# Padding the rows of the two stationary buffers of a float32r matmul kernel, from 256 to 272 and 260 columns a block

## What is computed

```python
u = rms_norm(x, norm_pre_mix)
proj = u @ w_in                                   # 2048 x 8512
q_sb, k_sb, v_sb, q_lat, kv_lat, k_r, gate_logits = split(proj)
y_sb  = stick_breaking_attention(q_sb, k_sb, v_sb) @ w_o_sb
y_mla = mla_attention(rms_norm(q_lat) @ w_uq, rms_norm(kv_lat) @ w_ukv, k_r) @ w_o_mla
mixed = (g_sb * y_sb + g_mla * y_mla) @ w_out     # g_* = sigmoid(gate_logits + b_gate)
h = x + rms_norm(mixed)
gu = rms_norm(h) @ w_gate_up                      # 2048 x 11264
h = h + rms_norm((silu(g) * up) @ w_down)         # 5632 x 2048
...
x = layer_norm(ALPHA * h + attention_mixer(h))    # h @ a_w_in, attention, @ a_w_out
x = layer_norm(ALPHA * x + retention_mixer(x))    # x @ r_w_in, retention, @ r_w_out
```

## Time and profile before

| | |
|---|---|
| Time, median of 3 runs | 2592.48 us (2590.3 to 2597.59) |
| Profiled execution: span from the first to the last instruction | 2588.1 us |
| Time of the profiled execution itself | not recorded apart from its span |
| TensorE busy, by the page | 2521.7 us, 97% |
| TensorE weight loads | 2088.9 us, 81% |
| VectorE | 1532.2 us, 59% |
| ScalarE | 1224.0 us, 47% |
| GpSimd | 56.7 us, 2% |
| Mean granted clock of TensorE | 0.992 |
| HBM traffic | 182 GB/s over the span |

### The profile page before, as it was taken

The page is one execution under the profiler, slowest core; times in us unless marked ns, Lnnn a source line. Parts: engine busy times, 40 slices in busy tenths (PEclk is TensorE's granted clock), DMA queues, the critical chain, the costliest instruction groups (busy, mean ns, idle before and its releaser), DMA issues.

```text
span 2588.1 us, 33845 instructions
## 1 busy us (share of the span) xinstructions
PE 2521.7 (97%) x11598; PEld 2088.9 (81%) x11598; DVE 1532.2 (59%) x2119; ACT 1224.0 (47%) x1543; POOL 56.7 (2%) x50
## 2 busy tenths in 40 slices
PE   8999999999999999999999999998999999999997
PEld 6888888787788888887888788877788888888785
DVE  5557656565744454445445787556756566666546
ACT  5455775544644444444444445543444444444442
POOL 0000000000100000000000100001000000000001
PEclk9999999999999999999999999999999999999998
DMA  8566555775465655555555554454555555555653
GB/s 269 173 189 184 172 184 165 244 238 181 161 201 186 190 189 188 190 189 179 187 188 170 177 187 143 126 179 155 179 171 187 173 178 181 172 178 174 211 188 121
DMA packets 215301, 472.19 MB, mean 182 GB/s; under 512 B 14688, under 2 KB 26016, under 8 KB 213920
## 3 DMA queue, kind: packets, MB, share of 16 engines
q1 hardware_dynamic: 205248, 445.70, 54.4%
q10 hardware_dynamic: 7904, 14.68, 1.6%
q0 software_dynamic: 2048, 10.53, 1.1%
HBM read 464.57 MB, written 6.29 MB: 182 GB/s over the span
## 4 chain that ended last, share of the span: by engine, by line
PE 90%; DVE 4%; ACT 2%; issue 2%; DMA 1%; ACTq 0%; DVEq 0%; SPq 0%; POOLq 0%
PE acc L430 25%; PE acc L432 25%; PE acc L431 25%; PE aux L430 5%; PE aux L431 5%; PE aux L432 5%; PE aux L451 1%; ACT whi L1012 1%; DMA raw<-w_o_sb 1%; DMA xT_raw<-xT 0%; DVE h L2239 0%; DVE stats L2227 0%; DVE wlo L1616 0%; DVE h L2217 0%; DVE rs_t L1667 0%
## 5 line engine op out<-in xcount | busy, mean ns | idle before, releaser
L1616 DVE TENSOR_TENSOR wlo<-raw,whi 128x1024 fp32r<-128x1024 f32 x840 | 1022.5, 1224 | 946.9 <-ACT whi L1012 942.4
L1012 ACT ACTIVATE whi<-raw 128x1024 fp32r<-128x1024 f32 x852 | 900.7, 1060 | 1194.7 <-PE acc L432 833.2
L430 PE MATMUL acc<-whi,xh 128*128 128x512 f32 (+1 forms) x2336 | 919.7, 394 | 15.2 <-DVE xl L1676 11.3
L432 PE MATMUL acc<-whi,xl 128*128 128x512 f32 (+1 forms) x2336 | 910.7, 390 | 0.0
L431 PE MATMUL acc<-wlo,xh 128*128 128x512 f32 (+1 forms) x2336 | 910.2, 390 | 0.0
L430 PEld LDWEIGHTS acc<-whi,xh 128*128 128x128 f32 x2336 | 440.7, 189 | 104.3 <-DVE xl L1676 11.7
L432 PEld LDWEIGHTS acc<-whi,xl 128*128 128x128 f32 x2336 | 440.4, 189 | 91.1
L431 PEld LDWEIGHTS acc<-wlo,xh 128*128 128x128 f32 x2336 | 441.1, 189 | 86.0
L430 PE MATMUL aux<-whi,osh 128*128 128x512 f32 x432 | 170.6, 395 | 3.5 <-DVE rgT L2320 0.9
L430 PE MATMUL acc<-whi,osh 128*128 128x512 f32 x432 | 171.2, 396 | 2.0 <-DVE s L2041 0.6
L432 PE MATMUL acc<-whi,osl 128*128 128x512 f32 x432 | 170.6, 395 | 0.0
(11 more groups left out here) (375 smaller groups left out, 1799.6 us busy)
## 6 DMA issues: line engine op xcount, KB each, us to landing
raw<-r_w_in SPq DMA_DIRECT2D x192, 512.0 KB, 3.6
raw<-w_gate_up SPq DMA_DIRECT2D x176, 512.0 KB, 3.4
raw<-w_in SPq DMA_DIRECT2D x112, 512.0 KB, 3.7
raw<-w_down SPq DMA_DIRECT2D x88, 512.0 KB, 4.6
raw<-a_w_in SPq DMA_DIRECT2D x80, 512.0 KB, 3.7
raw<-r_w_out SPq DMA_DIRECT2D x64, 512.0 KB, 4.5
raw<-w_out SPq DMA_DIRECT2D x32, 512.0 KB, 4.5
raw<-a_w_out SPq DMA_DIRECT2D x32, 512.0 KB, 4.6
```

Of the source, the lines that this page charges most:

```text
L430: pe.matmul(dst, lh, rh, start=start, stop=False, skip_group_check=True)
L432: return pe.matmul(dst, ll, rh, start=False, stop=stop, skip_group_check=True)
L1012: A(whi[:, slot], raw[:, slot], ACT.Copy).then_inc(hi_done, 1)
L1616: V.tensor_tensor(wlo[:, slot], raw[:, slot], f32(whi[:, slot]), ALU.subtract).then_inc(lo_done, 1)
```

## The change

The blocks of `xh` lie 272 columns (1,088 bytes) apart where they lay 256 (1,024 bytes) apart, those of `xl` 260 columns (1,040 bytes). The 256 columns in use, and every instruction and its shape, stay what they were; each access is made to the first 256 columns of a row. `xh` takes 17,408 bytes where it took 16,384, `xl` 16,640, so that `xl` starts 1,024 bytes later, and all that is put behind it, from `s0` to the last buffer, 1,280 bytes later. The order of the instructions on every engine is the same as before.

```diff
@@ -162,8 +162,8 @@
         raw = put("raw", [P, R, UE], F32)
         whi = put("whi", [P, R, UE], F32R)
         wlo = put("wlo", [P, R, UE], F32R)
-        xh = put("xh", [P, DK, TOK], F32R)
-        xl = put("xl", [P, DK, TOK], F32R)
+        xh = put("xh", [P, DK, TOK + 16], F32R)[:, :, 0:TOK]
+        xl = put("xl", [P, DK, TOK + 4], F32R)[:, :, 0:TOK]
         s0 = put("s0", [P, T, CW], F32)
         s1 = put("s1", [P, T, CW], F32)
         ident = put("ident", [P, P], F32)
```

## The result

The changed kernel takes 2619.92 us (median of 4 runs, 2618.38 to 2622.31) against 2591.72 us (4 runs) for the one before: a ratio of 1.0104, with a 95% interval of 1.0091 to 1.0117 (the two medians alone give 1.0109). It is 28.2 us slower, where 2627 us and +34.3 us were forecast. The profiled execution has a span of 2618.7 us, 30.6 more than before.

A forecast was written before the change was run, and what follows sets the result against it. TensorE's matmul pace was taken to bound the kernel; 6,020 loads leaving offset 0 at 5.7 ns gave +34.3 us, all else 0, so 2592.5 + 34.3 = 2626.8, say 2627 us; range 2550 to 2640 us.

The forecast's parts named there:

- TensorE's pace sets the end: Whole kernel: TensorE, busy 97% of the span, has its weights ready, so the end moves with its pace nearly one for one.
- The offset makes the difference between rows 5 and rows 6: Matmuls in `up` (`xh`, offset 0) against `down` (`osh`, 128 bytes): 226.7 against 232.4 ns, put down to the stationary block's offset.
- The witness of the earlier trace: 448-column matmuls on `xh`, offsets 0 and 256 in turn: 16.0 ns of extra, read as supporting a cost off offset 0.
- The first rival: Loads of `xh`, `xl`: distance or memory region counts instead of offset, so no change, 2592 us; chance 0.23.
- No other offset is quicker than 0: 512-column matmuls on `xh`, `xl`: every stretch leaving offset 0 has more than 13.3 ns of extra, so others cost more.
- The second rival: Loads of `xh`, `xl`: padding removes the 13.3 ns conflict, at most -80 us, 2512 us; chance 0.22.
- The count of loads and the price of 5.7 ns: 512-column matmuls on `xh`, `xl`: 6,020 loads leave offset 0 at 5.7 ns each, +34.3 us.
- the sign that blocks 0 and 8 keep the old pace: In `up` after the change: `kt` 0 and 8 alone keep the old pace only if each load acts for itself.
- `h0` at 384 acts as at 128: Matmuls on `osh`, `yTh`, `latTh`: `h0` moves from offset 128 to 384, taken as 0, bounds -17.5 to +17.5 us.
- The third rival: Only the shift of `h0` acts: `osh`, `yTh`, `latTh` fall to 226.7 ns, -17.5 us, 2575 us; chance 0.08.
- The load against the stream that runs beside it: Switches to and from `pth` in `ret`: a load's offset to the stream beside it counts, not the buffer; slow steps 0.24 us.
- The writers at 0: Writers of `xh` and `xl`, such as line 1979 with 673 ns: the longer step from block to block costs 0.

The follow-up runs named there:

- x_by_128: `xh` and `xl` begin 128 bytes later, unpadded, against the kernel before: 2626.86 us against 2590.90, ratio 1.0135.
- h0_even: 384 bytes left free ahead of `h0` in the kernel before, putting `osh`, `yTh`, `latTh` at offset 0: 2578.19 us against 2590.90, ratio 0.9951.
- all_by_64: 64 bytes left free ahead of `raw` in the kernel before, so every buffer moves together: 2591.30 us against 2590.90, ratio 1.0005.
- whi_by_128: 128 free bytes ahead of `whi` and 128 ahead of `wlo` in the kernel before, stationary buffers unpadded: 2602.79 us against 2591.51, ratio 1.0045.
- xh_272: Only `xh` padded to 272 columns, `xl` left at 256, against the kernel before: 2616.21 us against 2593.47, ratio 1.0093.
- xl_260: Only `xl` padded to 260 columns, with 256 free bytes behind it, against the kernel before: 2615.52 us against 2593.47, ratio 1.0083.
- xl_by_128: Only `xl` begins 128 bytes later, unpadded, against the kernel before: 2616.86 us against 2591.51, ratio 1.0101.

## Why the prediction was right

*TensorE's pace sets the end.* Right: of the 30.6 us by which the profiled span grew, 28.8 are in the steps on `xh` and `xl`; TensorE's waits for `xl` went from 15.1 to 14.8 us, and VectorE and ScalarE have the same busy time within 0.5 us. One line was misread on the way: the 833.2 us of ScalarE aren't the largest wait of that view. VectorE and GpSimd wait longer, for `whi` from ScalarE, which is itself behind TensorE's slots, so the conclusion stands.

```profile
POOL wlo L396 <- ACT whi L1012: 1002.8, 7, 737.7
DVE wlo L1616 <- ACT whi L1012: 942.4, 660, 8.4
ACT whi L1012 <- PE acc L432: 833.2, 540, 4.4
```

*The offset makes the difference between rows 5 and rows 6.* Right, and shown from four sides: `xh` and `xl` brought to the pace of `osh` by 128 bytes (x_by_128), `osh` brought to theirs by 384 (h0_even), everything moved together without effect (all_by_64), and the stream moved (whi_by_128, with an effect, though a smaller one than expected). The witness of the earlier trace rows isn't one: 256 bytes turned out to be free at 512 columns, and the 448-column steps at offset 0 take 202.7 ns and those at 256 take 202.6, so the 16.0 ns there aren't the price of leaving offset 0. The first rival, distance or region, falls with h0_even.

*No other offset is quicker than 0.* Right at 512 columns for those tried, 16, 32, 64, 128 and 256. The second rival, a padding that takes the 13.3 ns away, was not seen at any of them. Whether the 13.3 ns at offset 0 can go at all stays open, and 96, 160, 192 and 224 weren't tried. The rule of the Trainium skill that was weighed ("TensorE: Matmul & The Clock Gate", "Step-by-step: what each phase is for"), that loading the next weights doesn't take from the running matmul's reads, doesn't carry the conclusion drawn from it: 32 bytes of distance between load and stream cost 1.48%, so the address of the loaded block does matter. Whether it is read bandwidth that is lost isn't shown. The 215.7 ns at 512 columns stand in that same section as measured; the section "Back-to-back issue gap", which the prediction names for them, has some 216 ns by a formula for an isolated matmul and some 131 ns for a stream of loads and matmuls, and this trace, at 226.7 ns, agrees with neither.

*The count of loads and the price of 5.7 ns.* This term was mis-sized: the forecast has 34.3 us, the measurement 28.2. Two parts of its working were off, and that the sum came so near is partly luck. The modulus is 256 where the prediction took 512, so blocks 4 and 12 of `xh` are at a harmless distance, and the count of loads that leave offset 0 is 5,460 (4,480 x 12/16 and 2,100), not 6,020. And the price isn't one for each load: xh_272 and xl_260 cost 22.7 and 22.1 us and together 28.2. At 5.7 ns a load they would be 19.2 us (3,360 loads) and 12.0 us (2,100), together 31.1: the part of `xl` is taken at near half of what it costs alone, and in the change the costs of the two parts overlap, which the working doesn't have; the two errors nearly cancel. Whole buffers at one offset cost 36.0 to 36.5 us, 5.4 ns for each of the 6,720, near the 5.7 that was taken; the change, which moves the offset from block to block, has 4.2. Why the mixture is cheaper than the fixed offsets wasn't tried apart; in the trace of the change the sixteen blocks differ in `up`, from 226.7 ns a step for block 0, whose two parts are both at offset 0, over 231.4 for block 8, whose `xl` part is off by 128 bytes, to 234.4 for block 9. So the sign that blocks 0 and 8 keep the old pace if each load acts for itself held for 0 alone, and for 8 it was set wrongly; the clean case is xh_272, and there the blocks that are not off are slow.

*`h0` at 384 acts as at 128.* Right: 22.31 us in `down` before and after. The third rival needed the contrary.

*The load against the stream that runs beside it.* This reading of the earlier trace rows is half held, and the trace of before had the other half. At the switch to `pth` not one step is slow but two, 233 ns and then 231 by the trace's start times, before 226 follows:

```profile
1918.13 0.39 PE L430 MATMUL aux<-rvh,pth 128*128 128x512 f32 x1
1918.36 0.39 PE L431 MATMUL aux<-rvl,pth 128*128 128x512 f32 x1
1918.59 0.39 PE L432 MATMUL aux<-rvh,ptl 128*128 128x512 f32 x1
```

In the second of them `pth` is loaded while `rvh` streams, which are at offset 0 to each other; at the switch back it is the same, 233 and 231 ns. So a load that is off slows the step behind it too, as in xl_by_128, and a price for each load misses that. The streams' addresses matter, but the sizes in xl_by_128 (+25.4 us with one load in three off) and whi_by_128 (+11.3 with two in three) don't follow from it, nor do the steps by kind in either. Which pair of accesses meets, a load with the stream beside it, with the one behind it, or two neighbouring ones together, stays open.

*The writers at 0.* Right: line 1979 takes 673 ns before and after the earlier trace rows.

## What to carry to other kernels

When the other engines wait for TensorE and it hardly waits for them, look at the distance of neighbouring starts and compare it between phases that run the same shapes; a difference there points at addresses. In this kernel, at 512 columns, the starts of stationary and moving blocks want to be a multiple of 256 bytes apart within the partition: a few hundred bytes left free ahead of a buffer gave 0.5%, and a padding of 64 and 16 bytes a row took 1%. Padding rows wasn't neutral here.

## What the runs showed of the hardware

- A float32r matmul of 512 columns with a weight load of its own goes at 226.7 ns at the best offsets (0 and 256 bytes) and, when all loads are off by 32, 64 or 128 bytes, at 232.4 to 233.3 ns, at a mean granted clock of 0.99, the level of 2.4 GHz.
- The offset acts modulo 256 bytes: 256 gives 21.76 us for 96 steps, 128 gives 22.31 or 22.40, 64 and 32 give 22.40; 384 gives 22.31 on `osh`.
- At 16 bytes both paces occur in one execution, 21.76 and 22.40 us for 96 steps; each of 55 uninterrupted stretches keeps one of them.
- At 448 columns the pace doesn't follow the offset: 202.2 to 206.6 ns, and 202.7 and 206.0 in two kernels with the same offset (before, h0_even).
- One load in three off by 128 bytes (xl_by_128) costs 25.4 us, all three (x_by_128) 36.0: the load that is off runs in one kind of step, and two of the three kinds are slow (226.9, 232.5 and 234.0 ns).
